# Moving the start addresses of the activation buffers of a float32r kernel within a 128-byte unit

## The reference

```
def swiglu(u, wg, wu, wd):
    return (silu(u @ wg) * (u @ wu)) @ wd          # 1024 -> 2 x 2816 -> 1024

first block:   h += 0.5 * swiglu(rmsnorm(h));  mixer (pool, then latent attention);  h += 0.5 * swiglu(rmsnorm(h));   twice, then a norm
second block:  h += 0.5 * rmsnorm(swiglu(rmsnorm(h)));  mixer (stick-breaking attention with a convolution, then gated linear attention);  h += 0.5 * rmsnorm(swiglu(rmsnorm(h)));   twice
```

## Time and profile before

| | |
|---|---|
| median of 3 runs | 1979.84 us (1979.74 to 1982.69) |
| profiled execution, its own time | 1981.62 us |
| its span, first to last instruction | 1979.7 us |
| mean granted TensorE clock | 0.992 |
| PE busy | 1922.5 us, 97% |
| PE weight loads (beside PE) | 1768.1 us, 89% |
| DVE busy | 1230.5 us, 62% |
| ACT busy | 943.5 us, 48% |
| POOL busy | 61.7 us, 3% |
| moved from and to HBM | 338.94 MB, mean 171 GB/s |

### The profile page before, as it was taken

One profiled execution on the slowest core, in us unless ns is written; L12 is line 12 of the kernel. 1 busy time (PEld: TensorE's weight loads), 2 busy tenths in 40 slices (PEclk: granted clock), 3 DMA queues, 4 the chain that ended last, 5 costly groups with the idle time before them and its releaser, 6 DMA issues.

```text
span 1979.7 us, 33792 instructions
## 1 busy us (share of the span) xinstructions
PE 1922.5 (97%) x13276; PEld 1768.1 (89%) x13276; DVE 1230.5 (62%) x1651; ACT 943.5 (48%) x1291; POOL 61.7 (3%) x98
## 2 busy tenths in 40 slices
PE   7999999999999999999999998999999999989998
PEld 7999899989998988998999997899989998868997
DVE  5666765665555646666656597665565665767555
ACT  5444544454445645444544456644454446445443
POOL 0000100000000000000100000100000000020000
PEclk9999999999999999999999999999999999999999
DMA  6545455445453135444545333555445553324552
GB/s 259 187 184 191 149 203 189 182 152 195 185 192 126 65 139 202 186 182 184 198 185 190 149 128 107 222 195 191 181 173 194 186 190 115 130 107 180 191 191 96
DMA packets 61119, 338.94 MB, mean 171 GB/s; under 512 B 6816, under 2 KB 7200, under 8 KB 32640
## 3 DMA queue, kind: packets, MB, share of 16 engines
q1 hardware_dynamic: 59040, 330.00, 44.9%
q0 software_dynamic: 2016, 8.06, 1.1%
HBM read 336.98 MB, written 1.05 MB: 171 GB/s over the span
## 4 chain that ended last, share of the span: by engine, by line
PE 87%; DVE 7%; ACT 3%; issue 1%; DMA 1%; POOL 0%; SPq 0%; DVEq 0%; ACTq 0%
PE X L1454 54%; PE Y L1454 32%; DVE arena L1276 2%; DVE loA L977 1%; ACT hiA L536 1%; DVE xl L1004 1%; DMA rawA<-in_wa 1%; POOL rstd L441 0%; ACT xh L567 0%; DVE h L1037 0%; DVE xs L1030 0%; PE Y L1824 0%; PE X L1488 0%; DVE arena L1420 0%; PE X L1486 0%
## 5 line engine op out<-in xcount | busy, mean ns | idle before, releaser
L1454 PE MATMUL X<-xh,hiA 128*128 128x256 f32 x2592 | 728.9, 281 | 5.6 <-DVE xl L1004 5.2
L1454 PE MATMUL X<-xl,hiA 128*128 128x256 f32 x2592 | 725.5, 280 | 0.0
L1454 PE MATMUL X<-xh,loA 128*128 128x256 f32 x2592 | 724.7, 280 | 0.0
L977 DVE TENSOR_TENSOR loA<-rawA,hiA 128x2048 fp32r<-128x2048 f32 x221 | 506.3, 2291 | 284.4 <-ACT hiA L536 284.4
L1454 PEld LDWEIGHTS X<-xh,hiA 128*128 128x128 f32 x2592 | 489.6, 189 | 14.9 <-issue 3.9
L1454 PEld LDWEIGHTS X<-xl,hiA 128*128 128x128 f32 x2592 | 489.1, 189 | 6.6
L1454 PEld LDWEIGHTS X<-xh,loA 128*128 128x128 f32 x2592 | 489.1, 189 | 0.0
L536 ACT ACTIVATE hiA<-rawA 128x2048 fp32r<-128x2048 f32 (+1 forms) x234 | 424.3, 1814 | 70.2 <-PE Y L1454 39.6
L1454 PE MATMUL Y<-hiB,act_hh 128*128 128x512 f32 x704 | 279.3, 397 | 2.6 <-DVE act_hl L1090 2.6
L1454 PE MATMUL Y<-loB,act_hh 128*128 128x512 f32 x704 | 279.2, 397 | 0.0
L1454 PE MATMUL Y<-hiB,act_hl 128*128 128x512 f32 x704 | 279.2, 397 | 0.0
(11 more groups left out here) (239 smaller groups left out, 2062.7 us busy)
## 6 DMA issues: line engine op xcount, KB each, us to landing
rawA<-in_wa SPq DMA_DIRECT2D x221, 1024.0 KB, 5.5
rawB<-in_wb SPq DMA_DIRECT2D x181, 512.0 KB, 3.5
row_gain<-in_rows POOLq DMA_DIRECT2D x8, 512.0 KB, 7.3
arena<-in_gla POOLq DMA_DIRECT2D x1, 1280.0 KB, 10.2
h<-in_x SPq DMA_DIRECT2D x2, 512.0 KB, 4.7
rawA<-in_wa SPq DMA_DIRECT2D x2, 512.0 KB, 7.1
out<-h SPq DMA_DIRECT2D x2, 512.0 KB, 2.7
arena<-in_pool POOLq DMA_DIRECT2D x1, 768.0 KB, 8.5
```

Source lines behind the costliest of these rows:

```text
L977: nc.vector.tensor_tensor(loA[p][:, :], rawA[p][:, :], hiA[p][:, :].bitcast(f32), ALU.subtract).then_inc(a_lo, 1)
L1454: return say(nc.tensor.matmul(*args, **kw))
```

## The change

The diff changes three allocations of unused floats and nothing else. No instruction is added, taken away or moved on any engine; line numbers of all that follows grow by one.

```diff
         h = sb("h", [P, TT, D])
         xs = sb("xs", [P, TT, D])
-        half_line = sb("half_line", [P, 8])
+        line = sb("line", [P, 16])
         xh = sb("xh", [P, KD, TOKENS], f32r)
         xl = sb("xl", [P, KD, TOKENS], f32r)
+        line_2 = sb("line_2", [P, 16])
         act_s = sb("act_s", [P, 2, TOKENS])
         act_h = sb("act_h", [P, 2, TOKENS])
         act_hh = sb("act_hh", [P, 2, TOKENS], f32r)
...
         flag = sb("flag", [P, 2])
         act_warm = sb("act_warm", [P, 16])
-        half_line_2 = sb("half_line_2", [P, 8])
+        half_line = sb("half_line", [P, 24])
         ckvh = sb("ckvh", [P, TOKENS], f32r)
```

## The result

| | median | runs | span of the profiled execution |
|---|---|---|---|
| before | 1980.68 us | 6 (1979.74 to 1982.69) | 1979.7 us |
| after | 1987.58 us | 6 (1986.52 to 1989.09) | 1985.5 us |

The changed kernel is slower: ratio 1.0028, with a 95% interval from 1.0017 to 1.0038. The forecast was 1970, faster by 0.5%.

A forecast was written before the change was run, and what follows sets the result against it. PE's matmul starts were taken to bound the kernel: 1981.6 us profiled, less 9.5 for down, tokens and mixer 0, gives 1972.1; the median lies 1.8 lower, so 1970. Range 1930 to 1995, the forecast's own 1964 to 1974.

The forecast's parts named there:

- only the distance of PE's starts can change: Whole kernel: PE, busy 97%, sets the pace, so new addresses act through matmul start distances; other engines' effect taken as 0.
- the down term: 2112 down matmuls, moving 0 / stationary 32 becoming 0 / 0: 233.3 to 228.8 ns each, 9.5 us less.
- The hint from the gate sums: Gate sums, both operands starting at 32, took 227.5 and 230 ns against 233.3: equal offsets may be faster; no proof.
- The tokens' term: 9336 matmuls with tokens moving, 32 / 0 becoming 64 / 0: unchanged at 116.7 ns, 0; ends 72 us less, 10 more.
- the second rival: Gate, up and all products with tokens moving slow to 117.8 ns: 10.3 us more, 1990 without down gain; chance 0.22.
- The 528 mixer products: Mixer products with `xh` or `xl` stationary, 0 / 32 becoming 0 / 64: 0, at most 8 us less or 1 more.
- the earlier trace: Trace before the change: in `gla`, 90 matmuls of the same kind and offsets ran at 117.8 ns, the second rival's basis.
- The rival of no change: All matmuls: starts at 32, 64 or 0 all begin a line, so distances stay 116.7 and 233.3; 1979.8 us, chance 0.28.

The follow-up runs named there:

- matmuls alone: Programs without the kernel's computation that stream only its gate, up and down matmuls over stored numbers at chosen addresses; distances between starts were read, no kernel time.
- all at 0: The changed kernel's moved buffers all start at a multiple of 128, like the weights; 1996.23 us, ratio 1.0079 to the kernel before.
- products 128 on: The changed kernel with three small buffers moved so that the products lie 128 bytes further on; 1981.85 us, ratio 1.0004 to the kernel before.
- first run of matmuls alone: Only the kernel's matmuls, operands at chosen offsets within 128 bytes; behind six entry lengths, tokens at 32 gave 116.7 or 116.8 ns five times, 117.9 once.

## Why the prediction was wrong

*That only the distance of PE's starts can change* held. The counts of instructions are the same, DVE and ACT kept their busy times within 1 us, and the matmuls alone show the same distances with all other engines idle.

*The step that failed first is the down term*: "2112 x (233.3 - 228.8) = 9.5 us less". It measured 0.1 ns more in seven parts (by the median of their blocks) and 2.1 ns less in ffn2, together 264 x 2.1 - 1848 x 0.1 = 0.4 us less. The hint from the gate sums was true in kind: equal starts do give 226.6 to 229 ns (all at 0; products 128 on; matmuls alone). It was wrong that the change makes the starts equal. The table of offsets on which I argued counts bytes past 128, and the period is 256; by it the products went from 32 to 128 against the down weights, not to 0. At 128 matmuls alone had 231.5 ns; that seven parts of this kernel had 233.4 is a matter of the rhythms, which stay open. The addresses, and with them the 128, were there to be read before the run. `oh2` and `ol2`, 8192 bytes apart, were equal modulo 256 too.

*The tokens' term* was taken as 0 "between the ends". It measured 117.8 ns, the upper end, which is the second rival: 8280 x 1.1 = 9.1 us more outside ffn2, if all of them moved like the feed-forward parts, and in ffn2 half of 1056 at 117.8 and half at 113.5, 0.6 - 1.7 = 1.1 us less. The argument against an effect, that moving at 32 and moving at 0 have the same excess, compared two kinds of product (256 and 512 columns) as if the offset were the only thing between them. They do not have the same response: at equal starts one is near its worst, 120.0, and the other at its best, 226.6. The 528 mixer products, taken as 0 with them, did stay: 233.2 ns before and after.

The sum by the runs: 9.1 - 1.1 - 0.4 = 7.6 us; the medians differ by 6.9 and the spans of the profiled executions by 1985.5 - 1979.7 = 5.8. That the spans differ by less fits the stretches at a granted clock of 0.50 shown above, 1.5 us lost by the kernel before in its first down block and, by the changed one, 1.4 at the start of ffn2, with others on both sides. I gave the second rival 0.22 and worked its price out as 10.3 us; its condition, a difference of 64 in place of 32, and its size were right, and 117.8 ns was indeed the pace of the earlier trace rows. But that run had the offsets of all others (d = 32) and another rhythm, so that the same 117.8 came with the new difference is in part luck. One of six entries in the first run of matmuls alone did the same at d = 32, 117.9 ns, so it can be had without a change of offsets.

*The rival of no change* rested on all starts at a line's beginning being alike. The Trainium skill, "SBUF — State Buffer", specifications, gives cachelines of 16 bytes; starts at 0, 16, 32, 48, 64 and 80, all at the beginning of such a line, lie between 113.3 and 120.0 ns here, so that rule alone does not describe what PE sees. The Trainium skill, "TensorE: Matmul & The Clock Gate", back-to-back issue gap, gives columns / 2.4 GHz and 2.5 ns, from which 109.2 and 215.8 ns are estimates for 256 and 512 columns. The lowest steady distances in any run are 113.3 and 226.6, in both cases 17/16 of 106.7 and 213.3.

What stays open: why two rhythms exist at one pair of offsets and what picks one; and what in the memory repeats every 256 bytes. That PE's two reads, moving operand and weights, get in each other's way there would fit, since it is mostly the difference of their starts that counts; it was not shown, and no run left the weight loads out. For starts at odd multiples of 16 the difference is not all, as 0/16 gives 118.3 and 240/0 gives 117.1.

## What to carry to other kernels

Where PE is busy nearly all the time with float32r products, compare the distance between matmul starts with columns divided by the clock; here it held 9% of excess, and the start of one operand moved that, in matmuls alone, between 6.2% (113.3 ns) and 12.5% (120.0 ns). Sweep the offset of the moving operand against the stationary one over 256 bytes with the matmuls alone, in the kernel's own order and widths, since products of other shape want other offsets (112 for gate and up, 0 for down), and choose one whose distance is the same wherever it is tried (at 112 gate and up had 113.3 ns in two sweeps and behind eight entries). When an address is said to be a multiple of something, write out the full addresses before believing that it says enough.

## What the runs showed of the hardware that was not expected

- The distance of 256-column float32r matmuls with one weight load each depends on the starts of both operands in SBUF: 113.3 to 120.0 ns with tokens at multiples of 16 bytes and weights at 0, 123.1 with tokens at 4. It repeats with 256 bytes (64 and 320, 112 and 368, 624 and 1136).
- Of 512-column ones, weights moving at 0: 226.6 ns with products at 0, 120, 240 or 256, 228.8 at 192, 230.4 to 234.5 at the others tried.
- At the granted clock of 0.50, the same matmuls at d = 32 take 213 ns, with no excess.
- The granted clock falls to 0.50 in a few short stretches of an execution, in other places in the next one; a block of twelve down matmuls then took 4.42 us in place of 2.80.
- At some offsets two steady rhythms exist (113.3 or 117.8 at 64 and 192; 116.7 or 117.9 at 32; 116.7 or 118.7 at 16 and 144), each held to the end of a block; the kernel's alternating blocks in ffn2, 5.45 and 5.65 us, are both of them in turn.
- After a change from down to gate and up, the first 24 matmuls of a block can run slower than the rest, 114.9 against 113.3 ns at an offset of 112 with products at 0; in the kernel before and in the changed one, at 32 and 64, the halves are alike within 0.1 ns.
